# Second layer's w_out and ff1 products ahead of their norms; the first ff1 chunk in a buffer of its own; the context half of the input loaded ahead on SyncE's queue

## The reference

```
mod_x = silu(c) @ w_ada[l] + b_ada[l]          # sh1, sc1, g1, sh2, sc2, g2 = split(mod_x, 6)
hc = rmsnorm(h_ctx, g_pre_mix[l]) * (1.0 + csc1) + csh1
pc = hc @ w_in[l]                              # q, k, v, u, gate, fourier of the context
...                                            # attention, spatial gating, fourier mix
hx = rmsnorm(x, g_pre_mix[l]) * (1.0 + sc1) + sh1
px = hx @ w_in[l]
y = merge_heads(attn, sgu, four, g_mix[l], w_out[l])   # each part rmsnormed by itself, then @ w_out
x = x + g1 * rmsnorm(y, g_post_mix[l])
hx2 = rmsnorm(x, g_pre_ff[l]) * (1.0 + sc2) + sh2
x = x + g2 * rmsnorm(square(relu(hx2 @ w_ff1[l])) @ w_ff2[l], g_post_ff[l])
```

## Time and profile before

| | |
|---|---|
| median of 3 runs | 2383.97 us (2383.86 to 2388.11) |
| profiled execution, its own time | 2384.43 us |
| its span, first to last instruction | 2382.6 us |
| TensorE busy | 2286.0 us (96%) |
| VectorE, ScalarE, GpSimd busy | 811.3 (34%), 489.6 (21%), 145.7 us (6%) |
| granted TensorE clock, mean | 0.990 |
| DMA moved | 601.61 MB, mean 252 GB/s |

### The profile page before, as it was taken

The page is one execution under the profiler, slowest core; times in us unless marked ns, Lnnn a source line. Parts: engine busy times, 40 slices in busy tenths (PEclk is TensorE's granted clock), DMA queues, the critical chain, the costliest instruction groups (busy, mean ns, idle before and its releaser), DMA issues.

```text
span 2382.6 us, 34249 instructions
## 1 busy us (share of the span) xinstructions
PE 2286.0 (96%) x14400; PEld 1672.6 (70%) x14400; DVE 811.3 (34%) x2062; ACT 489.6 (21%) x1153; POOL 145.7 (6%) x150
## 2 busy tenths in 40 slices
PE   6989999999999999999999989999999999999998
PEld 4766888888887678887698855555555555555556
DVE  2245454578434420004674322222222222212224
ACT  3255410000023432101543210111111111111113
POOL 1000211144301000000000000000000000000000
PEclk9999999999999999999999989999999999999999
DMA  8722212134233344345333757999999999999993
GB/s 362 279 106 107 106 71 106 71 129 155 107 141 124 137 172 169 141 145 203 118 131 114 295 235 273 428 426 427 427 426 427 426 426 426 427 427 426 427 426 130
DMA packets 42262, 601.61 MB, mean 252 GB/s; under 512 B 4689, under 2 KB 5329, under 8 KB 5745
## 3 DMA queue, kind: packets, MB, share of 16 engines
q1 hardware_dynamic: 41616, 593.30, 61.4%
q10 hardware_dynamic: 480, 5.97, 0.6%
HBM read 598.20 MB, written 1.05 MB: 252 GB/s over the span
## 4 chain that ended last, share of the span: by engine, by line
PE 85%; DMA 10%; DVE 2%; ACT 2%; issue 1%; POOL 0%; SPq 0%; POOLq 0%; DVEq 0%; PEldq 0%; ACTq 0%
PE PS L1112 15%; PE PS L1136 8%; PE PS L866 8%; PE PS L641 7%; PE PS L676 6%; DMA RG<-in_w_up 6%; PE PS L625 6%; PE PS L728 5%; PE PS L516 4%; PE PS L615 3%; DMA BIG<-in_w_up 3%; PE PS L714 2%; PE PS L1041 2%; PE PS L1148 2%; PE PS L456 1%; PE PS L1107 1%
## 5 line engine op out<-in xcount | busy, mean ns | idle before, releaser
L2410 DVE TENSOR_SCALAR STAT<-PS 128x128 f32<-128x128 f32 (+1 forms) x128 | 37.8, 295 | 669.7 <-PE PS L1112 669.7
L1112 PE MATMUL PS<-BIG,XS 128*64 128x256 f32 (+1 forms) x2016 | 238.8, 388 | 3.3 <-DMA BIG<-in_w_up 3.3
L1112 PEld LDWEIGHTS PS<-BIG,XS 128*64 128x64 f32 (+1 forms) x2016 | 146.5, 139 | 93.8 <-issue 21.4
L1291 ACT ACTIVATE BIG<-PS 128x256 f32<-128x256 f32 (+2 forms) x205 | 85.7, 430 | 499.6 <-PE PS L641 138.9
L1112 PE MATMUL PS<-RG,XS 128*64 128x256 f32 (+1 forms) x1520 | 178.5, 385 | 5.3 <-DMA RG<-in_w_up 5.3
L866 PE MATMUL PS<-XS,RG 128*128 128x256 f32 x768 | 172.8, 383 | 5.0 <-DVE XS L1867 4.1
L866 PEld LDWEIGHTS PS<-XS,RG 128*128 128x128 f32 x768 | 146.3, 192 | 26.7 <-issue 6.9
L1112 PEld LDWEIGHTS PS<-RG,XS 128*64 128x64 f32 (+1 forms) x1520 | 108.3, 138 | 73.7 <-issue 15.6
L1716 ACT ACTIVATE STAT<-STAT 128x128 f32<-128x128 f32 (+1 forms) x128 | 40.1, 313 | 572.8 <-DVE STAT L2410 572.8
L1833 DVE TENSOR_SCALAR HOLD<-PS 128x256 f32<-128x256 f32 x27 | 11.4, 422 | 401.6 <-PE PS L492 301.4
L625 PE MATMUL PS<-HN,RG 128*128 128x256 f32 x640 | 142.0, 385 | 4.0 <-ACT HN L1338 4.0
(11 more groups left out here) (353 smaller groups left out, 3286.0 us busy)
## 6 DMA issues: line engine op xcount, KB each, us to landing
BIG<-in_w_up SPq DMA_DIRECT2D x64, 2048.0 KB, 27.1
RG<-in_w_up SPq DMA_DIRECT2D x48, 2048.0 KB, 27.9
RG<-in_w_ff SPq DMA_DIRECT2D x32, 2048.0 KB, 7.7
BIG<-in_w_down SPq DMA_DIRECT2D x32, 2048.0 KB, 29.3
RG<-in_w_ada SPq DMA_DIRECT2D x24, 2048.0 KB, 7.9
RG<-in_w_down SPq DMA_DIRECT2D x24, 2048.0 KB, 28.7
RG<-in_w_in SPq DMA_DIRECT2D x23, 2048.0 KB, 7.9
SM<-in_w_up SPq DMA_DIRECT2D x16, 2048.0 KB, 27.4
```

Of the source, the lines that this page charges most:

```text
L1112: i = pe.matmul(half_of(b, h, sides), Xg[:, k, 0:cap], w[:, k, h * wd:h * wd + wd], start=False, stop=k == 7)
L1291: i = act.activation(dst, banks[b][rows, part], fn)
```

## The change

1. **Input in halves.** `XS` is loaded as two transfers of 1024 KB, now on SyncE's queue: the context half behind the first 100 KB of `SM1`, the x half behind w_in's first chunk. `xs` in HBM is laid out anew, so that each half is 8 KB in one piece per partition there, and goes to 8 pieces of 1 KB in `XS`. Semaphore `s_in` becomes one for each.
2. **Start reordered.** On every engine the work on x's norm goes behind that of the context; each adaLN chunk is turned directly behind its row; the shifts of the context's first four tiles wait only for chunk 0, the other four for chunk 1; `w_in_halves` does k 0 to 3 of the four w_in tiles, then k 4 to 7 of the four.
3. **w_out in halves, second layer.** The products of tiles 0 to 3 with the Fourier and gating parts (four k of eight) come before the attention part's norm: tile 0 ahead of the last attention values, 1 and 2 ahead of the mean, 3 behind it. Their other halves follow.
4. **ff1's first chunk ahead of its norm, second layer.** `scaled_x` on ScalarE makes `XN`: x times the gain, and as column 256 the shift. `ff1_early` multiplies the four tiles with it, 257 columns; VectorE multiplies the result by r (1.0 for column 256) into `HE`, and ScalarE applies relu with column 256 as bias (`hidden_early`). The mean of squares becomes `mean_summed`, with six more additions on GpSimd. Chunk ("w_ff1", 1, 0) gets slot 8, a home in `BIG` where attention's probabilities were, free when the last `values` is done; the ring's next chunks move up by one.

The core of the diff:

```diff
+            if s == 8:
+                return BIG[:, 7680:7680 + CW]
...
+        XN, HE = view(BIG, 11776, 8, 257), view(BIG, 5632, 4, 257)
...
-                if new:
+                if new and key == ("w_ff1", 1, 0):
+                    slot = 8
+                    R.before[key], R.end[key], R.end["softmax"] = "softmax", through, ("o", 1, X, 7)
+                elif new:
...
+            def w_out_half(l, s, n, half):
+
+                w = chunk(("w_out", l, s, 0), ("y", l, s, 3)).rearrange("p (k n) -> p k n", k=8)
+                b = F.at["y", l, s, n][0] if half else take(("y", l, s, n))
+                for i in range(4 * half, 4 * half + 4):
+                    if n == 0:
+                        pe.wait_ge(s_mt, 8 * MIX[l, s] + i + 1)
+                    k = MERGE[i]
+                    m = pe.matmul(banks[b][:, 0:256], w[:, k, 128 * n:128 * n + 128], own(CAT, s)[:, k, :],
+                                  start=i == 0, stop=i == 7)
+                if half:
+                    m.then_inc(s_full[b], 1)
+
+            def ff1_early(tiles):
+
+                w = chunk(("w_ff1", 1, 0), ("h", 1, X, 3)).rearrange("p (k n) -> p k n", k=8)
+                b = [take(("h", 1, X, n)) for n in tiles]
+                for k in range(8):
+                    if tiles[0] == 0:
+                        pe.wait_ge(s_xn, k + 2)
+                    for n in tiles:
+                        m = pe.matmul(banks[b[n - tiles[0]]][:, 0:257], w[:, k, 128 * n:128 * n + 128], XN[:, k, :],
+                                      start=k == 0, stop=k == 7)
+                        if k == 7:
+                            m.then_inc(s_full[b[n - tiles[0]]], 1)
...
+            def w_in_halves(tiles):
+
+                w = chunk(("w_in", 0, C, 0), ("in", 0, C, 3)).rearrange("p (k n) -> p k n", k=8)
+                for half in range(2):
+                    for i in tiles:
+                        b = F.at["in", 0, C, i][0] if half else take(("in", 0, C, i))
+                        for k in range(4 * half, 4 * half + 4):
+                            if i == 0:
+                                pe.wait_ge(s_hn, NORM["mix", 0, C] + k + 1)
+                            m = pe.matmul(banks[b][:, 0:256], w[:, k, 128 * i:128 * i + 128], own(HN, C)[:, k, :],
+                                          start=k == 0, stop=k == 7)
+                        if half:
+                            m.then_inc(s_full[b], 1)
+                        elif i == 0:
+                            ada_turn(0, 1)
+                        if half and i == 1:
+                            mean_summed(("mix", 0, X), range(8), own(HN, X), ones)
...
             ada(0, 2)
             pe.wait_ge(s_const, 5)
-            ada(0, 3)
             mean_summed(("mix", 0, C), range(8), own(HN, C), ones)
             ada_turn(0, 2)
+            ada(0, 3)
             ada_turn(0, 3)
-            mean_summed(("mix", 0, X), range(8), own(HN, X), ones)
             ada(0, 0)
+            ada_turn(0, 0)
             ada(0, 1)
-            ada_turn(0, 0)
-            ada_turn(0, 1)
-            for i in range(12):
+            w_in_halves(range(4))
+            for i in range(4, 12):
...
+                if i == 8:
+                    w_out_half(1, X, 0, 0)
+            w_out_half(1, X, 1, 0)
+            w_out_half(1, X, 2, 0)
             merge("mA", 1, X)
-            for n in range(8):
+            w_out_half(1, X, 3, 0)
+            for n in range(4):
+                w_out_half(1, X, n, 1)
+            for n in range(4, 8):
                 w_out(1, X, n)
             mean_post("mix", 1, X)
             ada(1, 10)
             ada(1, 11)
             ada_turn(1, 10)
-            mean(("ff", 1, X), range(8), own(HN, X), ones)
+            ff1_early((0, 1))
             ada_turn(1, 11)
-            for c in range(8):
+            ff1_early((2,))
+            mean_summed(("ff", 1, X), range(8), own(HN, X), ones)
+            ff1_early((3,))
+            for c in range(1, 8):
...
-                if (kind, l) == ("mix", 0):
-                    act.wait_ge(s_mod, ADA[0, 1] + 1)
                 for k in range(8):
+                    if (kind, l, s) == ("mix", 0, C) and k % 4 == 0:
+                        if k:
+                            row(0, 1)
+                        act.wait_ge(s_mod, ADA[0, k // 4] + 1)
...
+            def scaled_x():
+
+                act.wait_ge(s_coef, GAIN[1, 2] + 1)
+                act.activation(XN[:, :, 256:257], mod(1)[:, 24:32, 0:1], ACT.Copy).then_inc(s_xn, 1)
+                for k in range(8):
+                    act.wait_ge(s_x, POST["mix", 1, X] + k + 1)
+                    act.activation(XN[:, k, 0:256], own(XS, X)[:, k, :], ACT.Copy, scale=coef(1, 2)[:, k, 0:1]).then_inc(s_xn, 1)
+                    act.activation(own(HN, X)[:, k, :], own(XS, X)[:, k, :], ACT.Square).then_inc(s_sq, 1)
+
+            def hidden_early(k):
+                f = own(FFH, X)[:, k, :]
+                freed(("h", 1, X, k))
+                S.up(act.activation(f, HE[:, k, 0:256], ACT.Relu, bias=HE[:, k, 256:257]))
+                act.wait_ge(s_act, S.n)
+                act.activation(f, f, ACT.Square).then_inc(s_ffh, 1)
...
             squares(0, C, "mix")
-            squares(0, X, "mix")
             row(0, 2)
             root(("mix", 0, C), C)
             row(0, 3)
-            root(("mix", 0, X), X)
             row(0, 0)
-            row(0, 1)
             shifted("mix", 0, C)
+            squares(0, X, "mix")
             for i in range(12):
...
-            squares(1, X, "ff")
+            scaled_x()
             row(1, 11)
             root(("ff", 1, X), X)
             shifted("ff", 1, X)
-            for k in range(32):
+            for k in range(4):
+                hidden_early(k)
+            for k in range(4, 32):
...
-            r[X] = rstd(("mix", 0, X), 1e-6, X)
             gain(0, 0, 1, "g_pre_mix", 1.0)
             dve.wait_ge(s_coef, 1)
             for s in C, X:
+                if s == X:
+                    turned(0, 0)
+                    turned(0, 1)
+                    dve.wait_ge(s_in[X], 16)
+                    r[X] = rstd(("mix", 0, X), 1e-6, X)
...
+            D.up(dve.memset(STAT[:, 256:257], 1.0))
             prenorm("ff", 1, X)
+            dve.wait_ge(s_dve, D.n)
+            for k in range(4):
+                b = full(("h", 1, X, k))
+                dve.tensor_tensor(HE[:, k, :], banks[b][:, 0:257], STAT[:, 0:257], ALU.mult).then_inc(s_free[b], 1)
...
+            pool.wait_ge(s_x, POST["mix", 1, X] + 8)
+            sums(("ff", 1, X), range(8))
...
+            sp.dma_start(own(XS, C), A["xs"][:, C]).then_inc(s_in[C], 16)
             early = [k for k in R.order if k in R.end]
             for i, key in enumerate(early):
                 if R.before[key]:
                     full(R.end[R.before[key]])
                 landing(key, source(key))
+                if key == ("w_in", 0, C, 0):
+                    sp.dma_start(own(XS, X), A["xs"][:, X]).then_inc(s_in[X], 16)
```

More of the change, by code:

```diff
@@ L96, in __init__ @@
     def __init__(self):
-        self.order, self.slot, self.nth, self.count, self.end, self.now, self.before = [], {}, {}, [0] * 8, {}, {}, {}
+        self.order, self.slot, self.nth, self.count, self.end, self.now, self.before = [], {}, {}, [0] * 9, {}, {}, {}
     def get(self, key, slot):
@@ L172, in build @@
         s_free = [sem(f"free{i}") for i in range(8)]
-        s_landed = [sem(f"landed{i}") for i in range(8)]
+        s_landed = [sem(f"landed{i}") for i in range(9)]
         s_used = sem("used")
-        s_cc, s_sm, s_in, s_sm2, s_sm3, s_out = (sem(n) for n in ("cc", "sm", "in", "sm2", "sm3", "out"))
+        s_cc, s_sm, s_sm2, s_sm3, s_out = (sem(n) for n in ("cc", "sm", "sm2", "sm3", "out"))
+        s_in = {X: sem("inx"), C: sem("inc")}
         s_const, s_mod, s_coef, s_kz = (sem(n) for n in ("const", "mod", "coef", "kz"))
```

20 lines of the change are left out of this document (9 added, 11 removed).

## The result

The changed kernel takes 2373.5 us (median of 8 runs, 2369.7 to 2377.3) against 2385.1 for the kernel before in the same job (8 runs, 2380.7 to 2392.2): a ratio of 0.995, 95% interval 0.9935 to 0.9964. That is a gain of 11.5 us (by the interval 8.6 to 15.5) where 18.1 were forecast, and 3.5 us above the end of the range; 1.1 of the 3.5 is that the kernel before was slower in this job than the 2384.0 that the forecast started from. In layer2_pad and after_pad, two kernels of the experiments, one execution of six each took 2620 and 2962 us, at a granted clock of 0.943 and 0.755 and for a reason that is not known: the ratios leave them out, the medians do not. Its local gains are there and a good part of them is gone again at the end.

A forecast was written before the change was run, and what follows sets the result against it. The prediction took TensorE's idle or slow stretches as the bound (85% of the chain, DMA 10%), treating two local problems plus a shift. Terms of -4.2, -3.0 and -10.9 gave -18.1 us: 2366 us, range 2363 to 2370.

The forecast's parts named there:

- It moves as a block: Expert stage, last 40% of the span: no instruction in it changes, so it only shifts, starting when earlier stages free buffers.
- Term 1: Start: w_in's first weights land at 31.0 us, tiles 0 to 3 done at 48.1 against 52.31: -4.2 us.
- A clock that falls elsewhere: Rival: a short new gap or other phase of attention gaps costs 1.7 to 3.3 us; 2367.7 to 2369.5; chance 0.16.
- Term 2: Second layer's w_out: -3.0 us, from 2.78 of waiting plus 1.6 lost to the clock, less 1.5 of idling.
- Term 3: Second layer's ff1: -10.9 us, from paced means 5.4, waiting 3.5, slow clock 3.3, less 0.9 and 0.5.
- What would show it: Signs: first w_in product near 31 us, second layer without long waits at clock 1.00, expert stage beginning 18 us earlier.

The follow-up runs named there:

- layer2_pad: Kernel before with only the second layer's part of the change, plus 128 waits (64 instructions) at the start of TensorE's program: 2369.3 us, ratio 0.9936.
- after_pad: The whole change plus 128 waits (64 instructions) at the start of TensorE's program, timed: 2368.0 us, ratio 0.9926 to the kernel before.
- before_pad: Kernel before plus 106 waits (53 instructions) at the start of TensorE's program: 2380.5 us, ratio 0.9986.
- pe_pad22: Changed kernel plus 22 waits (11 instructions) at the start of TensorE's program: 2376.3 us, ratio 0.9949 to the kernel before.
- pe_pad64: Changed kernel plus 128 waits (64 instructions) at the start of TensorE's program: 2365.8 us in one execution.
- start_only: Kernel before with only the start's edits (input in halves, norms reordered, w_in in halves): 2380.2 us, ratio 0.9978.
- wout_only: Kernel before with only the second layer's last two values and w_out products in halves: 2384.0 us, ratio 0.999.
- ff_only: Kernel before with only the second layer's first ff1 products ahead of the norm's mean: 2380.0 us, ratio 0.9976.
- pe_pad128: Changed kernel plus 256 waits (128 instructions) at the start of TensorE's program: 2361.3 us in one execution.

## Why the prediction was wrong

- **"It moves as a block"** is the step that failed. The prediction took the expert stage as rigid because no instruction in it changes. But the early ff1 products shorten TensorE's program ahead of it (24 rows fewer, one wait more), and the branch into expert 1's wide body takes some 3 us longer. Timed, the branch's price is 3.3 us in before (before against before_pad) and 5.7 to 7.4 in after, 2.4 to 4.1 us more; the intervals of these times leave about 6 us either way, so they don't settle it. The traces do. From expert 0's last products (1412.48 in before) to the last product of all TensorE runs the same work in every kernel, and it takes 968.6 to 970.9 us in the seven traces with the long branch (mean 969.2), 964.3 to 968.0 in the four with before's own code (965.9), 968.4 in pe_pad22 and 959.5 to 961.7 in the six with 53 instructions of waits or more (960.3). So the change lost 3.3 of the missing 6.6 us here. That the place decides is shown (pe_pad22, pe_pad64, and start_only and wout_only against ff_only). The dearer part is mostly wait: the branch itself is 2.8 us longer in the mean (6.5 us in the seven, 3.7 in the four), for a packet of code that starts later (last section). The clock matters more against the kernels with waits: in the 30 us from the branch on its mean is 0.82 in the seven, 0.87 in the four (0.77 to 0.94) and 0.98 in the six.
- **Term 1, the start (-4.2):** in the first trace of after each part came: weights at 31.51 (31.0 forecast), adaLN at 11.91 (11.3), no wait for the mean, release at 46.93 (48.1; the slow stretch that the old 15.8 held is missing). The packets under 2 KB did no harm that shows. But 46.93 is at the good end. In start_only w_in's weights land at 31.45 and its first four k run at half clock, 3.55 us instead of 1.99, so the release is at 48.42. Without the kernels of 53 instructions of waits or more, seven traces with the start's part have it at 46.9 to 48.8 (mean 47.9) and five without at 50.1 to 52.3 (mean 51.6): 3.7 us, 0.5 under the forecast. The shift then shrinks in the first layer's attention, where the clock falls now and did not before. Windows of before, then of after:

```profile
142.00:146.00 4.00, 3.49 (x17) 2.73 (x15) 0.47 (x2) 1.92 (x3) 0.00 (x0) 1.00 0.00 0
159.00:163.00 4.00, 2.20 (x13) 1.71 (x11) 0.00 (x0) 2.17 (x5) 0.00 (x0) 1.00 0.00 0
719.00:723.00 4.00, 2.62 (x12) 2.36 (x13) 0.55 (x2) 0.83 (x2) 1.05 (x2) 1.00 0.81 332
```

```profile
142.00:146.00 4.00, 4.00 (x18) 2.93 (x19) 2.22 (x7) 2.24 (x9) 0.00 (x0) 0.57 0.98 418
159.00:163.00 4.00, 3.92 (x16) 3.02 (x17) 2.40 (x7) 1.33 (x7) 0.00 (x0) 0.57 0.01 2
719.00:723.00 4.00, 4.00 (x12) 3.22 (x11) 2.81 (x7) 1.43 (x4) 0.00 (x0) 0.57 0.72 307
```

- Each of the three costs 1.7 us (4 us at 0.57). The first two are mostly the change's: between 130 and 170 us the clock is 0.91 in 9 of the 11 traces with the start's part (0.96 and 1.00 in the others; mean 0.92), and 1.00, 0.96, 0.91, 0.96, 1.00, 1.00, 0.96 in the seven without (mean 0.97). 0.05 of 40 us is 2 us. SyncE's issues say the same: the seven traces lead the five by 3.8 us at the issue near 119 us (before's time) and by 2.0 at the one near 172. So the rival *A clock that falls elsewhere* was real, in an unlooked-for place and beside the other loss.
- **Term 2, w_out (-3.0):** the mechanism came as written, with the wait of 1.58 (1.5 forecast). Its size is 2.8: the 1.6 us of slow clock in it was cover for the wait that comes next, as ff_only shows.
- **Term 3, ff1 (-10.9):** second chunk at 863.22 (863.1 without term 1's shift, which was down to 0.7 by then), pairs of 0.51 and 0.40 us, no late weights. The 3.3 us of slow clock in it were one execution's: between 845 and 875 us the six traces with the old ff1 have 0.89, 0.94, 1.00, 0.89, 0.89 and 0.89, so the average loss is 2.5 us; all twelve with the new have 1.00. (The term's parts add up to 10.8, not 10.9, and the rival of the clock to 2369.3, not 2369.5; nothing hangs on it.) Terms 2 and 3 together: 13.9 forecast, 13.0 in the traces of before and after (13.7 at 1337 less the 0.7 left of term 1), 11.9 timed with the branch short (about 7 to 17).
- The parts, as means over traces, add up to the size of the gap: 3.3 us from the branch on, 1.8 at 130 to 170, 0.8 of overrated clock, 0.5 of the start and 0.2 of term 2 are 6.6 of 6.6. That it comes out to the tenth is luck: the gain's own interval is 8.6 to 15.5 us, and the means rest on four to twelve traces. The router's slow clock (1.5 us in this pair, at 1386) is no part of it: between 1345 and 1400 us the clock's mean is 0.86 both over the twelve traces with the early ff1 products and over the six without.
- "What would show it" named three things to watch, and the third, the expert stage beginning 18 us earlier, did not come: the first expert began 13.5 us earlier, and the second 9.0. The range had no end for it: its widest allowance for the clock was 3.3 us and it had none for code.

## What to carry to other kernels

An edit that changes how many instructions an engine runs ahead of a data-dependent jump moves that jump within the engine's program. Before the rest is called rigid, look up the branches of the engine that sets the path (COMPARE_BRANCH rows in its queue), find the one that an idle TensorE product stands behind, and ask what it costs if it changes; where it is microseconds, try the same kernel with some harmless instructions at its head, and look whether the start still stands where it did. Compare such kernels from trace to trace over the stretch of unchanged work behind the branch: that was steady to a few us where the whole times were not. Credit slow clock only by its average over several executions, and only where no wait behind it takes up the slack.

## What the runs showed of the hardware

The length of one far branch of TensorE, by the places that it stands behind after's (counted in rows of the profile): 0: 6.4 to 6.8 us in six traces (ff_only 6.2); 11: 4.4; 23, before's own code: 3.5 to 3.9 in four; 64 or 76: 0.5 to 1.2 in five; 128: 0.5. A hint for it at 31 us, at 8 us, or none made no difference at 6.4 to 6.8 us. The other 31 rows of this branch take 63 to 88 ns.

What the branch waits for is a packet of code. One of 16 KB comes on the queue that brings it (q8), is on the way for 1.0 to 1.2 us, and in 17 of the 18 traces the branch ends 1.5 to 1.6 us after it has landed:

| | branch begins | code packet | branch ends |
|---|---|---|---|
| after | 1401.29 | 1405.36 to 1406.43 | 1407.91 |
| pe_pad22 | 1400.98 | 1402.70 to 1403.77 | 1405.35 |
| before | 1413.05 | 1414.27 to 1415.34 | 1416.92 |
| after_pad | 1401.96 | 1400.64 to 1401.69 | 1403.17 |
| pe_pad64 | 1399.14 | 1397.38 to 1398.43 | 1399.90 |

In pe_pad128 it has landed 2.4 us ahead of the branch, which then takes 0.5 us. So the place sets when this packet starts: 3.7 to 4.3 us behind the branch's beginning in the seven traces with the long branch, 1.0 to 1.2 behind it with before's own code, 1.3 to 3.4 ahead of it with 53 instructions of waits or more. "Runtime: NRT & Kernel Launch" of the Trainium skill (Instruction fetch mechanics) says that code comes in blocks of 256 instructions and that a taken branch to a target outside the two-page window must wait for a fetch. The traces agree on the block (16 KB for about 250 rows) and on the wait for it, with none for the 31 other rows; they add that the packet can be under way before the branch comes, and then little is left to wait. Why it starts up to 4 us behind the branch in one place and ahead of it in another was not tried and stays open.

The granted clock makes most of the spread. In one job's 40 executions of before, 2377.6 to 2390.6 us go with means from 0.993 down to 0.986 or 0.987, about 1.6 us for each 0.001. The means of before (0.990) and after (0.990, 14 executions) are the same, though the change took away the slow stretches of the second layer; at 130 to 170 us the mean fell from 0.97 to 0.92, and behind the branch it is no higher than before.
